# Two transformer blocks with a mixture of experts on one core: eighteen ring slots, another routing order, each combine between gate and up products

## The reference

```python
g_idx = argmax(t @ rg_w + rg_b)                    # 4 groups
e_logits = (t @ re_w[g] + re_b)[g_idx]             # 8 experts in the chosen group
top_v, top_i = top_k(e_logits, 2)
weights = softmax(g_logits)[g_idx] * softmax(top_v)
expert_ids = g_idx * 8 + top_i                     # 32 experts, 2 for each token
# for each expert e, of the tokens that chose it:
hid = silu(x @ wg[e]) * (x @ wu[e])                # 1024 -> 512
y  += weights * (hid @ wd[e])                      # 512 -> 1024
out = rmsnorm(h + y, norm_final_w)
```

## Time and profile before

| | us |
|---|---|
| median of 3 runs | 1323.53 (1322.75 to 1326.82) |
| profiled execution | 1326.84, its span 1325.2 |
| PE busy | 1283.0 (97%) |
| PEld busy | 969.9 (73%) |
| DVE busy | 588.9 (44%) |
| ACT busy | 470.3 (35%) |
| POOL busy | 64.9 (5%) |
| DMA | 349.35 MB, mean 264 GB/s |

### The profile page before, as it was taken

How to read it: one execution, slowest core, us unless ns; L and a number is a source line. 1 busy time by engine, 2 the same in 40 slices (tenths; PEclk the granted TensorE clock), 3 DMA queues, 4 the chain that set the end, 5 groups by cost and what they waited for, 6 DMA issues and landing times.

```text
span 1325.2 us, 19228 instructions
## 1 busy us (share of the span) xinstructions
PE 1283.0 (97%) x8372; PEld 969.9 (73%) x8372; DVE 588.9 (44%) x939; ACT 470.3 (35%) x698; POOL 64.9 (5%) x68
## 2 busy tenths in 40 slices
PE   8999999999999999999999999999999999999996
PEld 7887898999998889979999998834344343443432
DVE  3576656444556576495555656522011110111112
ACT  4543555434444644444654454311011010110102
POOL 4021000000001021010200000000000000000000
PEclk9999999999999999999999999999999999999999
DMA  9786336555443534453345559489999999999995
GB/s 351 279 281 245 141 127 232 183 190 191 173 157 111 185 127 159 135 176 128 103 163 179 185 178 378 174 349 421 421 420 421 421 421 421 419 421 421 421 420 213
DMA packets 102548, 349.35 MB, mean 264 GB/s; under 512 B 6114, under 2 KB 9472, under 8 KB 77888
## 3 DMA queue, kind: packets, MB, share of 16 engines
q1 hardware_dynamic: 100912, 345.56, 68.8%
q0 software_dynamic: 1376, 2.50, 0.8%
q10 hardware_dynamic: 176, 0.07, 0.0%
HBM read 347.05 MB, written 1.05 MB: 263 GB/s over the span
## 4 chain that ended last, share of the span: by engine, by line
PE 82%; DVE 7%; DMA 6%; ACT 3%; issue 1%; DVEq 0%; ACTq 0%
PE bank L551 42%; PE bank L938 14%; PE bank L973 7%; DMA weights<-in_expert_w_up 4%; PE bank L789 3%; PE bank L748 3%; PE bank L474 2%; DVE WHL L1411 2%; DMA arena<-in_expert_w_up 2%; PE bank L578 2%; PE bank L508 1%; ACT WHL L992 1%; PE bank L518 1%; PE bank L689 1%; PE bank L715 1%
## 5 line engine op out<-in xcount | busy, mean ns | idle before, releaser
L551 PE MATMUL bank<-XH,WHL 128*128 128x256 f32 x2928 | 541.8, 285 | 7.6 <-DVE WHL L1411 3.8
L551 PEld LDWEIGHTS bank<-XH,WHL 128*128 128x128 f32 x2928 | 462.7, 193 | 12.6 <-DVE WHL L1411 5.5
L551 PE MATMUL bank<-XL,WHL 128*128 128x256 f32 x1464 | 415.6, 284 | 0.0
L1411 DVE TENSOR_TENSOR WHL<-weights,WHL 128x1024 fp32r<-128x1024 f32 x223 | 282.8, 1285 | 213.5 <-ACT WHL L992 213.1
L992 ACT ACTIVATE WHL<-weights 128x1024 fp32r<-128x1024 f32 x223 | 231.9, 1054 | 215.8 <-PE bank L551 209.6
L551 PEld LDWEIGHTS bank<-XL,WHL 128*128 128x128 f32 x1464 | 282.7, 193 | 0.1
L938 PE MATMUL bank<-arena 128*64 128x512 f32 x512 | 142.1, 593 | 2.6 <-DMA arena<-in_expert_w_up 2.6
L938 PE MATMUL bank<-weights,arena 128*64 128x512 f32 x384 | 113.6, 593 | 5.1 <-DMA weights<-in_expert_w_up 5.1
L551 PE MATMUL bank<-WHL,XH 128*128 128x512 f32 x320 | 102.4, 394 | 4.1 <-DVE WHL L1411 4.1
L938 PEld LDWEIGHTS bank<-arena 128*64 128x64 f32 x512 | 45.2, 137 | 72.2 <-issue 67.2
L2112 DVE SCALAR_TENSOR_TENSOR chainm<-bank,small,chainm 128x512 f32<-128x512 f32 x16 | 12.0, 751 | 182.9 <-PE bank L938 182.9
(11 more groups left out here) (347 smaller groups left out, 1219.2 us busy)
## 6 DMA issues: line engine op xcount, KB each, us to landing
weights<-in_w_in SPq DMA_DIRECT2D x58, 1024.0 KB, 5.1
arena<-in_expert_w_gate SPq DMA_DIRECT2D x32, 1024.0 KB, 19.6
arena<-in_expert_w_up SPq DMA_DIRECT2D x32, 1024.0 KB, 22.7
arena<-in_expert_w_down SPq DMA_DIRECT2D x32, 1024.0 KB, 26.1
weights<-in_expert_w_up SPq DMA_DIRECT2D x24, 1024.0 KB, 24.7
weights<-in_expert_w_down SPq DMA_DIRECT2D x24, 1024.0 KB, 24.4
weights<-in_expert_w_gate SPq DMA_DIRECT2D x24, 1024.0 KB, 20.9
weights<-in_w_ada SPq DMA_DIRECT2D x22, 1024.0 KB, 7.5
```

The lines of the kernel that those rows point to most:

```text
L551: ins = e.matmul(o, l, r, start=first, skip_group_check=True, stop=g.part == g.parts - 1 and k == g.kc - 1 and n == 2)
L1411: e.tensor_tensor(lo, unit_weights(g, u), hi, ALU.subtract).then_inc(S.w_lo, 1)
```

## The change

The kernel after differs in these points.
- The ring has 18 slots: one more of `arena`, and `hT`, once the router's logits are done. For this `hp`, `hpT`, y and `wpick` get one buffer each, `frow` (the last norm's weights, broadcast) moves in three pieces to `spare` and the end of `maskf`, and its transfers wait on POOL for the first block's norm.
- Routing: `direct` (1,024 elements, place times expert, for the first four experts) and one sum make all of the first `pick`; `inpair` is computed after the first choice. The rows for `low_rows` are put in chunk order by two more copies of ScalarE. `spin(7, 32)` becomes `spin(7, 15)`.
- `turn_weights(p)` and `combine(p - 1)` stand between gate and up products for p > 0.
- In the last pair the down weights' last quarter is loaded by itself: pieces 190 and 191 are half as long, and 192 and 193 hold the rest.
- VectorE copies bank 6 to y as soon as bank 6 is complete; the last norm is ordered in halves.

```diff
-        wpT = [hT[:, i, :] for i in range(2)]
+        wpT = [chainm[:, HID + i * T:HID + (i + 1) * T] for i in range(2)]
-        wpick = [hT[:, 2 + i, :].rearrange("p (j s) -> p j s", j=TT) for i in range(2)]
+        wpick = maskf[:, HID:HID + T].rearrange("p (j s) -> p j s", j=TT)
+        frow = [spare[:, 0:512], spare[:, 512:768], maskf[:, 768:1024]]
-        hp = [chainm[:, i * HID:(i + 1) * HID] for i in range(2)]
-        hpT = [maskf[:, i * HID:(i + 1) * HID].rearrange("p (k s) -> p k s", k=4) for i in range(2)]
+        hp = chainm[:, 0:HID]
+        hpT = maskf[:, 0:HID].rearrange("p (k s) -> p k s", k=4)
...
+            def turn_weights(p):
+                clear(6)
+                w.wait_ge(S.m_slots, weighed(p))
+                for j in range(TT):
+                    ins = e.transpose(bank[6][:, j * P:(j + 1) * P], wpick[:, j, :], ident[:, :])
+                ins.then_inc(S.m_wt, 1)
+                free[6] = (S.m_wc, p + 1)
...
-            spin(7, 32)
+            spin(7, 15)
             choose(0)
             for p in range(NPAIR):
                 for wi in range(2):
...
                     free[b] = (S.m_h2 if wi else S.m_h1, p + 1)
+                    if wi == 0 and p:
+                        turn_weights(p)
+                        combine(p - 1)
                 if p == 1:
                     clear(6)
                     w.wait_ge(S.ov_v, 3)
                     e.matmul(bank[6][:, 0:2], ones[:, :], over[:, 0:2], start=True, stop=True).then_inc(S.ov_p, 1)
                     free[6] = (S.ov_v, 4)
-                clear(6)
-                w.wait_ge(S.m_slots, weighed(p))
-                for j in range(TT):
-                    ins = e.transpose(bank[6][:, j * P:(j + 1) * P], wpick[p % 2][:, j, :], ident[:, :])
-                ins.then_inc(S.m_wt, 1)
-                free[6] = (S.m_wc, p + 1)
-                if p:
-                    combine(p - 1)
+                if p == 0:
+                    turn_weights(0)
                 clear(7)
                 w.wait_ge(S.m_h2, p + 1)
...
-                            x = moe_load(p, 2, half, s_)
+                            alone = p == NPAIR - 1 and k == 3
+                            x = 12 * NPAIR + s_ if alone else moe_load(p, 2, half, s_)
...
             for j in range(TT):
                 e.activation(by_chunk(uhi)[:, j, :, :], xtok2[:, j, :].rearrange("p (q k) -> p q k", k=KC),
                              ACT.Copy).then_inc(S.rn, 1)
+            for j in range(TT):
+                e.activation(by_chunk(full)[:, j, :, :], xtok2[:, j, :].rearrange("p (q k) -> p q k", k=KC),
+                             ACT.Copy).then_inc(S.rn, 1)
...
             def low_rows(j):
-                w.wait_ge(S.rn, j + 1)
-                e.tensor_tensor(ulo[:, j, :].rearrange("p (k q) -> p k q", k=KC),
-                                xtok2[:, j, :].rearrange("p (q k) -> p k q", k=KC),
-                                uhi[:, j, :].bitcast(F32).rearrange("p (k q) -> p k q", k=KC),
-                                ALU.subtract).then_inc(S.rl, 1)
+                w.wait_ge(S.rn, TT + j + 1)
+                e.tensor_tensor(ulo[:, j, :], full[:, j, :], uhi[:, j, :].bitcast(F32), ALU.subtract).then_inc(S.rl, 1)
...
-            then(e.tensor_tensor(inpair, ph.unsqueeze(2).broadcast_to([P, two, 2, CAP]),
-                                 par.unsqueeze(3).broadcast_to([P, two, 2, CAP]), ALU.mult))
+            then(e.tensor_tensor(direct, ph.unsqueeze(2).broadcast_to([P, two, 4, CAP]),
+                                 dv[:, :, 0:4].unsqueeze(3).broadcast_to([P, two, 4, CAP]), ALU.mult))
             last()
-            for p in range(2):
-                slots_of(p, pick[:, :, p * P:(p + 1) * P], pair)
+            by_rank = direct.rearrange("p (j r) e s -> p j r (e s)", r=2)
+            e.tensor_tensor(pick[:, :, :], by_rank[:, :, 0, :], by_rank[:, :, 1, :], ALU.add).then_inc(S.m_slots, 1)
+            nslots[0] += 1
             for j in range(TT):
                 low_rows(j)
             chosen(0)
+            then(e.tensor_tensor(inpair, ...))
...
-                w.wait_ge(S.m_dn, 8 * p + 8)
-                if p >= 2:
-                    w.wait_ge(S.m_cb, 4 * (p - 1))
-                e.tensor_copy(yo[p % 2][0], bank[6][:, :]).then_inc(S.m_yv, 1)
+                w.wait_ge(S.m_dn, 8 * p + 6)
+                if p:
+                    w.wait_ge(S.m_cb, 4 * p)
+                e.tensor_copy(yo[0], bank[6][:, :]).then_inc(S.m_yv, 1)
...
             added(1, 1)
-            scaled(0)
+            inverted(0)
+            times_row(0, 0)
             summed(1)
-            scaled(1)
+            times_row(0, 1)
+            inverted(1)
+            times_row(1, 0)
+            times_row(1, 1)
...
+            w.wait_ge(S.fin, KC)
+            for f_, (c0, c1) in zip(frow, FROW):
+                e.dma_start(f_, a["norm_final_w_2"][c0:c1]...)
...
-        arena_ring = [(arena[:, ARENA - (8 - i) * SLOT:ARENA - (7 - i) * SLOT], sem(f"arena_slot{i}_loaded"),
-                       (S.x_lo, 86 if i == 7 else 78), None) for i in range(8)]
-        moe_ring = arena_ring[0:7] + [(base_slots[:, (nload + i) % RING, :], s_slot[(nload + i) % RING], None,
+        arena_ring = [(arena[:, ARENA - (9 - i) * SLOT:ARENA - (8 - i) * SLOT], sem(f"arena_slot{i}_loaded"),
+                       (S.x_lo, 86 if i == 8 else 78), None) for i in range(9)]
+        moe_ring = arena_ring[0:8] + [(base_slots[:, (nload + i) % RING, :], s_slot[(nload + i) % RING], None,
                                        (nload + i) % RING) for i in range(RING)]
+        moe_ring += arena_ring[8:] + [(late[:, i, :], sem(f"late_slot{i}_loaded"), (S.mm, len(units)), None) for i in range(2)]
+        moe_ring += [(hT[:, :, :].rearrange("p k t -> p (k t)"), sem("h_slot_loaded"), (S.lg, TT), None)]
```

More of the change, by code:

```diff
@@ L252, in build @@
         w8 = b5.take([P, KC])
-        frow = b5.take([P, D])
         tri = b5.take([P, P])
@@ L425, in build @@
         S.hg_n, S.hg_g = sem("hg_normed"), sem("hg_gated")
-        S.wm = sem("norm_weights")
         S.r1, S.rs2 = sem("first_norm_sum"), sem("second_norm_sum")
         S.u2, S.fin_a, S.fin_v, S.fin = (sem("first_norm_" + n) for n in ("u", "rms", "rstd", "out"))
-        S.zz, S.z, S.dec_a, S.dec_v, S.gb = (sem("gla_" + n) for n in (
-            "gate_pe", "gate", "decay_act", "decay_dve", "decay_sum"))
+        S.zz, S.z, S.dec_a, S.dec_v = (sem("gla_" + n) for n in (
+            "gate_pe", "gate", "decay_act", "decay_dve"))
         S.oGn = sem("gla_normed")
@@ L788, in combine @@
                         clear(b)
-                    e.matmul(bank[b][:, :], wpT[p % 2][:, j * P:(j + 1) * P], yo[p % 2][n],
+                    e.matmul(bank[b][:, :], wpT[p % 2][:, j * P:(j + 1) * P], yo[n],
                              start=p == 0, stop=p == NPAIR - 1, skip_group_check=True).then_inc(S.m_cb, 1)
@@ L970, in tensor @@
                         for s_ in range(2):
-                            x = moe_load(p, 2, half, s_)
+                            alone = p == NPAIR - 1 and k == 3
+                            x = 12 * NPAIR + s_ if alone else moe_load(p, 2, half, s_)
                             w.wait_ge(*moe_landed(x))
-                            ins = e.matmul(bank[6 + n][64 * s_:64 * s_ + 64, :], hpT[p % 2][:, k, 64 * s_:64 * s_ + 64],
-                                           moe_weights(x, 2, D)[:, kk, n * 512:(n + 1) * 512], start=k == 0, stop=k == 3)
+                            ins = e.matmul(bank[6 + n][64 * s_:64 * s_ + 64, :], hpT[:, k, 64 * s_:64 * s_ + 64],
+                                           moe_weights(x, 2, D)[:, 0 if alone else kk, n * 512:(n + 1) * 512],
+                                           start=k == 0, stop=k == 3)
                             if kk == 1:
@@ L1376, in scalar @@
                 w.wait_ge(S.m_ht, p + 1)
-                if p >= 2:
-                    w.wait_ge(S.m_dn, 8 * (p - 1))
-                e.activation(hpT[p % 2], bank[7][:, :].rearrange("p (k s) -> p k s", k=4), ACT.Copy).then_inc(S.m_hc, 1)
+                if p:
+                    w.wait_ge(S.m_dn, 8 * p)
+                e.activation(hpT, bank[7][:, :].rearrange("p (k s) -> p k s", k=4), ACT.Copy).then_inc(S.m_hc, 1)
                 if p % 2 and p + 1 < NPAIR:
@@ L2050, in vector @@
             chosen(0)
+            then(e.tensor_tensor(inpair, ph.unsqueeze(2).broadcast_to([P, two, 2, CAP]),
+                                 par.unsqueeze(3).broadcast_to([P, two, 2, CAP]), ALU.mult))
             then(e.tensor_tensor(eg, gl, gmax.broadcast_to([P, TT, 4]), ALU.subtract))
@@ L2140, in scaled @@
                 w.wait_ge(S.rstd, NORMS + j + 1)
-                for n in range(2):
-                    c = slice(n * 512, (n + 1) * 512)
-                    e.scalar_tensor_tensor(out=normed[:, j, c], in0=xtok2[:, j, c], scalar=sj, in1=frow[:, c],
-                                           op0=ALU.mult, op1=ALU.mult).then_inc(S.t_out, 1)
```

(13 more changed lines are left out.)

86 lines of the change are left out of this document (47 added, 39 removed).

## The result

22 executions of each kernel gave a median of 1329.06 us after (1324.89 to 1331.85) and 1326.8 us before (1322.65 to 1327.33). The ratio is 1.0030, 95% interval 1.0022 to 1.0039: the change made the kernel 0.3% slower, some 4 us. The medians alone lie 2.3 us apart and the means 3.2; executions of one kernel spread over 5 to 7 us, so 2 to 4 us is what the times can say. The forecast was +0.2 us, a median of 1323.8 with a range from 1314 to 1328, and the measured median lies 5.3 us above the forecast. Of these, 3.3 us are the base: the three runs of before that were known had their median at 1323.53, the 22 have it at 1326.8. The other 2 us are the change. In the measurements beside the experiments one execution of before took 2863.98 us and is left out of the ratios.

The account below looks back on a forecast made before the run. In the expert stage transfers and TensorE's work were taken as close bounds, with TensorE setting the end after the change. -3.8 - 11.8 + 16.2 - 0.4 = +0.2 us gave a median of 1323.8, 8-in-10 range 1314 to 1328.

Parts of the forecast that it names:

- Routing, 3.8 us: Before the first gate: 15 idle products instead of 32 let the choice of rows start 3.8 us earlier, bounds 2.9 and 3.8.
- Rival B: In routing: VectorE ends last, so the choice starts no earlier; if all is lost +3.8 us, 1327.6; chance 0.06.
- Waits for DMA, 11.8 us: Expert stage, pairs 10 to 15: TensorE's waits for weight transfers, 11.8 us in all, would all go.
- Together 1.15 us for each of the pairs 2 to 15: After up products: 0.87 us exposed wait for VectorE plus 0.28 restart of transposes, 16.1 us over 14 pairs.
- the upper bound of 1.32: Expert stage, per pair: all that pair 0 differs from pair 2 taken as the wait's price, 18.5 us in all.
- Pair 1: Second expert pair: already pays 1.02 us for a wait for VectorE, would pay 1.15 later, so 0.1 us more.
- rival C: Expert stage: TensorE's clock falls after the new idle gaps, 1.6 us a fall, +24 in 15 pairs, 1348; chance 0.04.
- The tail, 0.4 us: End of kernel: VectorE's y copy starts when bank 6 is full, before the down products end, gaining 0.4 us.
- an estimate of 0.97 us a pair: Expert stage: 0.80 wait plus 0.17 restart from the skill's page, 13.6 us in all, time 2.5 us lower; not adopted.
- The base: Starting time: profiled execution of before, 1326.84, lies 3.3 above the median 1323.53, so the forecast became 1323.8 instead of 1327.0.
- Rival A: Expert stage: the engine's queue covers the wait for VectorE, so DMA rules; 13.0 us less, 1310.5; chance 0.14.

Follow-up runs that it names:

- the move alone: Kernel before with only the turned weights and combine moved between gate and up products, 16 slots and 32 idle products kept: ratio to before 1.0061.
- the longer wait: Kernel after with one more VectorE op ahead of each pair's product of gate and up, TensorE's wait 1.43 instead of 0.83 us: ratio to before 1.0168.
- the kernels that do hide the wait: Kernel after with the combine's fourth product and the turn behind up: in all pairs, 0.9923 of before; in the last only, other combines wholly behind up, 0.9891.
- the gap filled: Kernel after with three idle TensorE products behind each pair's up products, from the second pair on, during the wait for VectorE: ratio to before 1.0032.

## Why the prediction was wrong

The mechanism was right, and two sizes were off: the price of a pair (1.15 us, measured 1.31) and the base (1323.53, measured 1326.8). A third term, the clock, stood at nothing. By the forecast's own terms:

- **Routing, 3.8 us.** 3.80. Rival B, that this would be lost, did not happen.
- **Waits for DMA, 11.8 us.** All gone, and the transfers have more cover than needed; two slots less change nothing.
- **"Together 1.15 us for each of the pairs 2 to 15."** This is the step of the change's sum that failed: it is 1.31, x 14 = 18.3 instead of 16.1, +2.2. I took the end of up products from pair 1's row, 13.78, in which gate and up run without a break. Behind a combine they take 13.94. Pair 0's own row of 13.94 stood beside it, and the upper bound of 1.32, made from it, was the right value: pair 0's gate too comes behind products that fill the whole array (the norms' sums, L776).
- **Pair 1.** 31.32 - 31.04 = 0.28 instead of 0.1.
- **The clock.** Nothing in the sum, a fall at each pair in rival C. The truth is one fall of 1.2 us in the stage, in three profiles of this order of work and in the move alone; none in the stage of before. All four falls come in an odd pair (13, 13, 11, 13), behind the one gap of 0.83 us, and none in an even pair, where 0.83 and 0.65 follow each other; why there is not shown. The Trainium skill ("TensorE: Matmul & The Clock Gate", section "HAM oscillation — how this bites in real kernels") describes a kernel that waits for a transfer behind each burst of products, for longer than any wait in this stage, and falls back to the half rate each time. With the longer wait the trace comes near that, in eight pairs of sixteen; with 0.83 us it does not.
- **The tail, 0.4 us.** 0.9: the last combine starts with the end of the down products, and the wait for y (0.77) is gone whole.
- **The base.** "It lies 3.3 above the median of 1323.53, so the median forecast is 1323.8." Three runs were too few. The 22 executions of before fall in two groups, 8 from 1322.65 to 1323.91 and 14 from 1326.02 to 1327.33, and two of the three known ones were of the lower group. The profiled execution, 1326.84, was an ordinary one, and nothing should have been taken off: -3.3, the largest part of the miss in the time.

The sum of the change, without the base: 0.2 + 2.2 + 0.2 + 1.2 - 0.5 = +3.3, against +3.4 in the chain. That lies at the top of the forecast's own range, +3.5, and near the 4 us that it gave as the least a measurement can tell. The rule of the Trainium skill that I had weighed ("TensorE: Matmul & The Clock Gate", section "Single matmul latency"; an estimate of 0.97 us a pair) would have been further off; the measured restart of the transposes is 0.28 us, not 0.17.

Rival A, in which the wait is hidden, was wrong about this kernel and right about the price: -13.0 forecast, and the kernels that do hide the wait come to -11.3 and -12.2 by the chain.

Open: what sets the spread of several us among executions of one kernel. Each profile shows falls of the clock in the first blocks (windows under 0.97 near 16, 172, 420, 540 and 680 us), two to five of them, in before and after alike. Each costs 1.7 us of full clock, so 3.4 to 8.5 us in sum, and they are not the same ones each time. The start of the idle products moves with their number in the 14 profiles: 845.8 to 845.9 with two, 846.4 to 848.9 with three, 850.0 to 850.1 with four, 850.2 with five. The two first profiles have four and three, which by this count is 1.7 of their 3.3 us. The mean granted clock of every execution is on record too, and points the same way: for the kernel after run again, spans go from 1324.4 us at 0.996 to 1330.4 at 0.991. So the spread goes with the granted clock; where the falls lie in the executions that were not profiled, and why one has more of them, is not shown.

## What to carry to other kernels

When two bounds lie within 3% of each other (here 440.7 us of TensorE's work and 452.46 with transfers), work out both sums, transfers and engine, for each edit: two slots were worth 5 us or nothing, and moving a block of products cost 13 us or saved 2, by which of them held in that place. A block of independent products behind a result that another engine must finish is cover; before it is moved for the sake of one pair at the end, move it in that pair alone. A wait of known length needs only as much work behind it as it is long: 1.23 us of 3.8 was enough here. A base of three runs can sit in the wrong one of two groups: look at the profiled execution too before taking it for the exception. And where the price of a thing can be read from two rows, ask which of them has the same neighbour: the row after a change of product shape was the right one.

## What the runs showed of the hardware

- A group of 64-column products behind 128-column ones takes 0.15 to 0.20 us more than behind its own kind (7.02 and 7.07 against 6.87 for 32).
- The clock fell behind gaps as short as these: 1.4 and 0.65 us with four transposes between cost it in eight pairs of nine (1.7 us of longer down products each), 1.4 us followed by 5 us of products in none of seven, and 0.83 us followed by the same products in one odd pair of the stage (1.2 us) in each of four profiles. No single rule of the gaps' length or number fits all three.
- In the profile with the gap filled, the queue for instructions moved a second packet after the last store was issued. In the DMA view of that kernel from 1318 us on, and then of the kernel after:

```profile
q8 instruction: 2, 0.03, 0.7%
```

```profile
q8 instruction: 1, 0.02, 0.3%
```

Over the whole execution it moves 67 packets there and 66 in each of the 13 other profiles. The chain ends as it does in the kernel after, yet the span goes on 2.9 us longer. This would fit code that is loaded once more at the end because the program has grown. That is not shown: one profile has it, and it was not tried by itself.
